# Moving the second layer's split activation tiles by other byte offsets than 192

## The reference

```python
for l in range(DEPTH):                      # DEPTH = 2
    xn  = rmsnorm(h,  norm1_g[l]) * (1 + sc1)  + sh1
    xnc = rmsnorm(hc, norm1_g[l]) * (1 + sc1c) + sh1c
    # token_mix: x @ w_in (pool | hyena | q | kv | three gates), three branches,
    # each gated by a sigmoid and summed, then @ w_out
    h = h + g1 * token_mix(xn @ w_in[l], k_c, v_c, lp, cos, sin)
    h = h + g2 * sq_relu_mlp(rmsnorm(h, norm2_g[l]) * (1 + sc2) + sh2, w_ff1[l], w_ff2[l])
    if not last:                            # the same for hc, with the context's vectors
        hc = ...
return rmsnorm(h, final_g)

def sq_relu_mlp(x, w1, w2):                 # w1 1024 x 4096, w2 4096 x 1024
    return jnp.square(jax.nn.relu(x @ w1)) @ w2
```

## Time and profile before

| | us |
|---|---|
| median of three runs | 1437.91 |
| the three runs | 1441.01, 1436.75, 1437.91 |
| time of the profiled execution | 1435.72 |
| its span, first to last instruction | 1433.8 |
| PE busy in the span | 1386.6 (97%) |
| DVE, ACT, POOL busy | 760.0, 545.1, 199.3 |

### The profile page before, as it was taken

How to read it: one execution, slowest core, us unless ns; L and a number is a source line. 1 busy time by engine, 2 the same in 40 slices (tenths; PEclk the granted TensorE clock), 3 DMA queues, 4 the chain that set the end, 5 groups by cost and what they waited for, 6 DMA issues and landing times.

```text
span 1433.8 us, 19717 instructions
## 1 busy us (share of the span) xinstructions
PE 1386.6 (97%) x8132; PEld 1128.3 (79%) x8132; DVE 760.0 (53%) x1091; ACT 545.1 (38%) x843; POOL 199.3 (14%) x185
## 2 busy tenths in 40 slices
PE   8999999999999999999999999979999999999997
PEld 4558756777777887777778888858769989899997
DVE  5445665234444475644223443465866767775664
ACT  5633363232231232433112331133465435553552
POOL 1151000613001143000000002200005212300012
PEclk9999999999999999999999999989999999999998
DMA  9232302444631255244443235322415736555552
GB/s 376 113 136 88 118 16 103 169 147 148 247 119 44 74 213 198 76 160 147 147 176 104 93 110 218 122 82 95 140 40 189 264 130 208 179 191 191 179 191 72
DMA packets 55770, 208.43 MB, mean 145 GB/s; under 512 B 6294, under 2 KB 6678, under 8 KB 54145
## 3 DMA queue, kind: packets, MB, share of 16 engines
q1 hardware_dynamic: 52992, 194.22, 39.0%
q0 software_dynamic: 2688, 12.95, 2.4%
HBM read 203.48 MB, written 3.67 MB: 144 GB/s over the span
## 4 chain that ended last, share of the span: by engine, by line
PE 90%; DVE 4%; ACT 3%; issue 1%; DMA 1%; SPq 0%; POOL 0%; DVEq 0%; ACTq 0%
PE ps L1472 26%; PE ps L1474 25%; PE ps L1473 25%; PE ps L1768 2%; PE ps L1501 2%; PE ps L1866 1%; PE ps L1876 1%; PE ps L1619 1%; PE ps L1779 1%; PE ps L1792 1%; DMA pairs<-in_pairs 1%; DVE rstd L1046 1%; DVE wl L1009 1%; PE ps L1724 1%; DVE normed L1068 0%
## 5 line engine op out<-in xcount | busy, mean ns | idle before, releaser
L1472 PE MATMUL ps<-xh,wh 128*128 128x512 f32 (+2 forms) x1392 | 473.8, 340 | 13.0 <-DVE cql L1100 9.8
L1009 DVE TENSOR_TENSOR wl<-raw,wh 128x1024 fp32r<-128x1024 f32 (+2 forms) x272 | 355.1, 1308 | 235.4 <-ACT wh L708 232.3
L1473 PE MATMUL ps<-xl,wh 128*128 128x512 f32 (+2 forms) x1392 | 466.7, 335 | 0.0
L1474 PE MATMUL ps<-xh,wl 128*128 128x512 f32 (+2 forms) x1392 | 466.4, 335 | 0.0
L708 ACT ACTIVATE wh<-raw 128x1024 fp32r<-128x1024 f32 (+2 forms) x272 | 283.6, 1043 | 316.3 <-PE ps L1474 315.7
L1472 PEld LDWEIGHTS ps<-xh,wh 128*128 128x128 f32 (+1 forms) x1392 | 261.1, 188 | 53.0 <-issue 20.6
L1473 PEld LDWEIGHTS ps<-xl,wh 128*128 128x128 f32 (+1 forms) x1392 | 262.8, 189 | 28.4 <-issue 1.3
L1474 PEld LDWEIGHTS ps<-xh,wl 128*128 128x128 f32 (+1 forms) x1392 | 261.3, 188 | 29.1
L1472 PE MATMUL ps<-hid_h,wh 128*128 128x512 f32 (+1 forms) x512 | 172.5, 337 | 0.0
L1473 PE MATMUL ps<-hid_l,wh 128*128 128x512 f32 (+1 forms) x512 | 171.7, 335 | 0.0
L1474 PE MATMUL ps<-hid_h,wl 128*128 128x512 f32 (+1 forms) x512 | 171.6, 335 | 0.0
(11 more groups left out here) (237 smaller groups left out, 1435.0 us busy)
## 6 DMA issues: line engine op xcount, KB each, us to landing
raw<-in_units SPq DMA_DIRECT2D x262, 512.0 KB, 3.3
mod_ring<-in_mod_units SPq DMA_DIRECT2D x49, 512.0 KB, 4.0
gap_hy<-in_mod_units SPq DMA_DIRECT2D x15, 512.0 KB, 5.0
pairs<-in_pairs SPq DMA_DIRECT2D x6, 1024.0 KB, 14.5
gap_relu<-in_mod_units SPq DMA_DIRECT2D x7, 512.0 KB, 4.5
filters<-filt POOLq DMA_DIRECT2D x10, 256.0 KB, 2.7
filt<-filters POOLq DMA_DIRECT2D x2, 1280.0 KB, 10.4
ftab<-in_fwd POOLq DMA_DIRECT2D x3, 768.0 KB, 5.2
```

The lines of the kernel that those rows point to most:

```text
L1009: dve.tensor_tensor(wl[:, g % SLOTS, 0:n], raw[:, g % SLOTS, 0:n], wh[:, g % SLOTS, 0:n].bitcast(F), ALU.subtract)\
L1472: pe.matmul(dst, w_h, m_h, start=first, stop=False)
L1473: pe.matmul(dst, w_h, m_l, start=False, stop=False)
L1474: return pe.matmul(dst, w_l, m_h, start=False, stop=last)
```

## The change

Layer 0's views stay where they are. Layer 1's views had all been 48 floats (192 bytes) into their rooms. Now the high and low tiles of each pair begin at different offsets:

| tiles | before, bytes | after, bytes (high, low) |
|---|---|---|
| xh, xl | 192, 192 | 160, 224 |
| fh, fl | 192, 192 | 224, 160 |
| hid_h, hid_l | 192, 192 | 176, 208 |

```diff
-SHIFT = 48
 ROOM = 64
...
-        xh_of = by_layer(ctx, "xh", KB, (0, SHIFT))
-        xl_of = by_layer(ctx, "xl", KB, (0, SHIFT))
+        xh_of = by_layer(ctx, "xh", KB, (0, 40))
+        xl_of = by_layer(ctx, "xl", KB, (0, 56))
...
-            fh_of = by_layer(s, "fh", 4, (0, SHIFT))
-            fl_of = by_layer(s, "fl", 4, (0, SHIFT))
+            fh_of = by_layer(s, "fh", 4, (0, 56))
+            fl_of = by_layer(s, "fl", 4, (0, 40))
...
-            hid_h_of = by_layer(s, "hid_h", 16, (0, SHIFT))
-            hid_l_of = by_layer(s, "hid_l", 16, (0, SHIFT))
+            hid_h_of = by_layer(s, "hid_h", 16, (0, 44))
+            hid_l_of = by_layer(s, "hid_l", 16, (0, 52))
```

## The result

| | before | after |
|---|---|---|
| median, us | 1438.81 (7 runs, 1436.75 to 1441.58) | 1446.40 (7 runs, 1442.21 to 1447.10) |
| ratio after to before | | 1.0045, 95% interval 1.0033 to 1.0056 |
| profiled execution: time, span | 1435.72, 1433.8 | 1446.92, 1444.8 |

The change made the kernel slower, by 0.45% or about 6.5 us (the means of the seven runs, 1439.0 and 1445.4, differ by 6.4, the medians by 7.6). The forecast was 1431.4.

A forecast was written before the change was run, and what follows sets the result against it. PE was taken to bound the kernel. The profiled 1435.7 us less 6.5 for the MLP gives 1429.2; the runs' median lies 2.2 higher, so 1431.4. Range 1424 to 1447, likeliest case 1428 to 1433.5.

The forecast's parts named there:

- The bound: Whole span: PE is 90% of the last-ending chain, so changes in matmul spacing reach the end one to one.
- the writers: ACT and DVE, writing the shifted tiles at other offsets, mostly beside PE; costed at nothing.
- That addresses alone can change the step: Full-clock 256-column matmuls show steps of 113.3, 117.8 and 120.0 ns where only addresses differ or a stop came before.
- The value taken: Layer 1's MLP: 487 triples gain 13.3 ns each, 6.5 us less; states elsewhere stay mixed as before.
- short step: Smallest spacing of 256-column matmuls, seen in layer 1's gates and pool: 113.3 ns, 340.0 a triple.
- The argument from the parts: All three pairs: spreading high and low part changes the relation that differs between weight-load lines L1472 and L1473, one slow.
- middle state: Layer 1's MLP and some other stretches: 117.8 ns a matmul, 353.3 a triple, one weight load at 192 ns.
- The draw: PE's state after the stop at 1250 us decides one run of 487 triples; a flip is worth 6.5 us.
- no difference: Rival: stops, not shifts, draw the states, so the same mix returns; 1438, within 4.3 us; chance 0.25.
- The slower rival: All three pairs: streams beginning inside a 64-byte piece need 17, long step becomes steady; 8.5 us loss, 1446.4; chance 0.30.
- The fetch by 64 bytes: Inferred from three triple times, 51, 53 and 54 multiples of 6.67 ns, the time of 64 bytes of each row.
- What would show it: Layer 1's MLP, 1250 to 1422 us: right if steps 113.3 and loads 188 ns; slower if 120 and loads 192.

The follow-up runs named there:

- e5: Kernel before with a 64-byte pad moving wh, wl and all later tiles; layer 1 xh, xl and hid_h, hid_l at 0, fh, fl at 192: 1450.08 us, ratio 1.0078.
- e11: Kernel before with a 64-byte pad ahead of wh and xh, xl moved along, so every distance to the weights is kept: 1437.42 us, ratio 1.0001.
- e3: Kernel before with layer 1 xh, xl at 0, fh, fl at 64, hid_h, hid_l at 128 bytes: 1447.75 us, ratio 1.0060.
- e6: Kernel before with layer 1 xh 64, xl 192; fh 192, fl 64; hid_h, hid_l both 64 bytes: 1442.28 us, ratio 1.0025.
- e4: Kernel before, unchanged, run again with a second profile: 1439.32 us, ratio 1.0001.
- e10: Kernel before with layer 1 hid_h, hid_l at 64 bytes in place of 192: 1439.39 us, ratio 1.0007.
- e2: Kernel before with layer 1 xh 192, xl 128; fh 128, fl 192; hid_h 128, hid_l 256 bytes: 1446.07 us, ratio 1.0044.
- e1: Kernel before with layer 1 xh, xl and fh, fl all at 160, hid_h, hid_l both at 176 bytes: 1443.55 us, ratio 1.0028.
- e13: Kernel before with a 64-byte pad between wh and wl, moving wl and all later tiles; layer 1 fh, fl at 128 bytes: 1450.26 us, ratio 1.0083.

## Why the prediction was wrong

**The bound, right.** PE's steps come through one to one: 6.0 us by steps, 6.5 measured. That the writers cost nothing fits with it; no run tested them alone.

**That addresses alone can change the step, right.** The 120 of uq against the 113 of the gates was read rightly as a matter of where the tile stands against the weights: e5 and e11 show it for `xh`. The Trainium skill, in "TensorE: Matmul & The Clock Gate", Part 2, has weights and moving operand come through independent read ports. The runs do not bear out that nothing is lost by it: where the moving tile stands against the weights costs up to 6.7 ns a matmul, between distances 192 and 0. That the loss arises between those two reads is inferred from the distances that count; no run isolates them. The other users of these buffers are ACT and DVE, which write them. Against these speaks that the step is even over more than a hundred triples, while DVE and ACT are busy for 53% and 38% of the span; it was not tested.

**The value taken, wrong.** The step that failed reads: "The short step in the MLP and the states elsewhere as mixed as before". I took the short step from distance 192 and assumed that it stays reachable at other distances. But it was found only where both parts stand at the same odd multiple of 64 bytes: 192, and 64 in e3. At 0, 128, 160, 176, 184 and 188, and with parts apart, no stretch had it. So the change took away 340.0 wherever it occurred and gave 355.4 to 356.0. In the terms of the sum: the MLP's 487 triples, put at 6.5 us less, cost 1.2 more, and the stretches elsewhere, put at nothing, cost 4.8 (3.3 of them for the 212 that had been short).

**The argument from the parts, wrong.** Spreading high and low part was to undo the one slow load of the middle state. e6 shows that spreading alone removes the short step.

**The draw, half right.** States are drawn by stops, and e4 and e10 show it for the gates. But the one draw at 1250 us on which the forecast hung came out middle in all eight profiles in which `xh` and `xl` are 192 from the weights. Nor is it the only such place: the 31 triples of `xh` from 1024 us of the kernel before (later by up to 18 us in the others) are middle in all eight, the 23 from 1107 us short in all eight. At these stops the draw is no even chance, so the argument that three quarters of the triples in the middle state were "more than a fair draw would give" had no ground. As the states elsewhere vary only in some stretches, "no difference" could not come true once no short step was left.

**The slower rival, right in direction, wrong in cause.** It gave 8.5 us at a steady 120.0 for the 17th piece. The step became 118.5 to 118.7, and whole pieces elsewhere (e2, e3) lose as much, so the number of pieces is not the cause. That its time equals the measured median is chance. Nor did the gain of half a piece for `hid`'s parts appear: 356.0 a triple. The fetch by 64 bytes, inferred from three numbers, is not borne out either: 351.9, 354.6, 356.0 and 357.8 a triple (e1, e13, e3, e1) are no whole multiples of 6.67.

**What would show it, right but for one mark.** The steps told the cases apart. The weight loads did not: those of ff2a after take 188 to 189 ns at a step of 118.7. Weight loads of the kernel after in ff2a, layer 1:

```profile
L1471 PEld LDWEIGHTS ps<-hid_h,wh 128*128 128x128 f32 x128 | 24.1, 188 | 0.0
L1472 PEld LDWEIGHTS ps<-hid_l,wh 128*128 128x128 f32 x127 | 24.0, 189 | 0.0
L1473 PEld LDWEIGHTS ps<-hid_h,wl 128*128 128x128 f32 x127 | 24.0, 189 | 0.0
```

Open: why 64 and 192 are good and 128 bad with 256 columns, and 0 good and 32, 128 and 192 bad with 512; and what selects the middle state in the MLP.

## What to carry to other kernels

Where float32r matmuls of 256 columns follow each other with a new block of weights each, read the distance between starts and not the duration: a few bytes of address can move it between 113 and 120 ns. Compare it with that of another tile of the same shape, and count how the states change at stops, before any change of addresses is judged. A step seen at one placement is evidence for that placement alone; a placement that is good for one width has to be tried again for the other.

## What the runs showed of the hardware

- The step of a 256-column float32r matmul with its own weights, by distance from the weights in bytes (both parts alike, means in ns): 0: 120.0; 64: 113.3 or 117.8; 128: 118.7; 160: 117.3 or 118.7; 176: 119.3; 184: 120.0; 188: 115.6 or 120.0; 192: 113.3 or 117.8. With 160 and 224, or 176 and 208, for the two parts: 118.5 to 118.7.
- With 512 columns: 0: 226.7; 32 and 192: 233.3; 128: 232.4 or 233.3; 0 from `wh` and 192 from `wl`: 231.1.
- One program at one placement has several steady states, which were seen to change only where PE stops or goes on to another tile: 340.0 and 353.4 a triple for the same stretch in two executions.
- The kernel before, unchanged, ran from 1435.8 to 1441.5 in one batch of ten, and the granted clock in layer 0 differed between two profiles (0.97 and 0.93 in the first 100 us) though nothing there had been changed.
